# The first modulation group in two halves of the features, with two weight chunks loaded in between and the first products drawn forward

## What is computed

```
mod = silu(c) @ w_mod[i] + b_mod[i]          # six groups of 1024; c for latent tokens, c_ctx for context
h   = rmsnorm(x, g_mix_pre) * (1 + mod[1]) + mod[0]
p   = h @ w_in[i]                            # then decays, attention, Fourier mixing, convolution
```

## Time and profile before

| | |
|---|---|
| median of three runs | 1592.35 us |
| lowest, highest | 1590.29, 1592.84 us |
| the profiled execution | 1594.53 us, span 1592.7 us |
| PE busy | 1536.5 us, 96% |
| VectorE, ScalarE, POOL busy | 855.0, 571.8, 593.4 us |
| mean DMA rate | 115 GB/s |

### The profile page before, as it was taken

The page is one execution under the profiler, slowest core; times in us unless marked ns, Lnnn a source line. Parts: engine busy times, 40 slices in busy tenths (PEclk is TensorE's granted clock), DMA queues, the critical chain, the costliest instruction groups (busy, mean ns, idle before and its releaser), DMA issues.

```text
span 1592.7 us, 22922 instructions
## 1 busy us (share of the span) xinstructions
PE 1536.5 (96%) x9056; PEld 1383.9 (87%) x9056; DVE 855.0 (54%) x1309; ACT 571.8 (36%) x923; POOL 593.4 (37%) x309
## 2 busy tenths in 40 slices
PE   5999999999999999999999989999999999999997
PEld 2799999887799999999999869888898888888887
DVE  1576888637756325761366684477666332223236
ACT  4644214525544213441244255432535322222221
POOL 0532212245425525553255233332252444444441
PEclk9899999999999999999999999999999999999999
DMA  9544532255312203122121441663050333323221
GB/s 369 205 157 150 160 112 91 82 200 197 134 57 77 80 26 106 54 80 79 53 80 60 143 168 53 206 199 111 28 169 22 114 117 114 125 92 104 94 83 63
DMA packets 54062, 183.93 MB, mean 115 GB/s; under 512 B 5650, under 2 KB 10642, under 8 KB 51028
## 3 DMA queue, kind: packets, MB, share of 16 engines
q1 hardware_dynamic: 47826, 168.85, 31.5%
q10 hardware_dynamic: 6146, 13.83, 2.5%
HBM read 171.13 MB, written 11.53 MB: 115 GB/s over the span
## 4 chain that ended last, share of the span: by engine, by line
PE 90%; DVE 3%; ACT 3%; DMA 1%; POOL 1%; issue 1%; SPq 1%; ACTq 0%; DVEq 0%; POOLq 0%
PE A L1063 62%; PE A L1318 8%; PE N L1318 4%; PE G L1318 4%; PE A L1252 1%; PE A L1246 1%; PE G L1221 1%; DMA raw<-modw 1%; PE G L1373 1%; PE G L1180 1%; PE A L1214 1%; PE N L1234 1%; PE A L1260 1%; PE N L1164 1%; SPq L916 1%
## 5 line engine op out<-in xcount | busy, mean ns | idle before, releaser
L1000 POOL TENSOR_TENSOR w_lo<-raw,w_hi 128x1024 fp32r<-128x1024 f32 (+2 forms) x163 | 385.8, 2370 | 659.8 <-ACT w_hi L1400 622.0
L1063 PE MATMUL A<-h_hi,w_hi 128*128 128x512 f32 (+2 forms) x1264 | 415.1, 359 | 20.6 <-POOL h_lo L1046 11.0
L1063 PE MATMUL A<-h_hi,w_lo 128*128 128x512 f32 (+2 forms) x1264 | 404.2, 350 | 0.0
L1063 PE MATMUL A<-h_lo,w_hi 128*128 128x512 f32 (+2 forms) x1264 | 404.1, 350 | 0.0
L1400 ACT ACTIVATE w_hi<-raw 128x1024 fp32r<-128x1024 f32 (+2 forms) x163 | 167.3, 1028 | 371.4 <-PE A L1063 330.5
L1063 PEld LDWEIGHTS A<-h_hi,w_hi 128*128 128x128 f32 x1264 | 234.8, 190 | 64.4 <-POOL h_lo L1046 17.4
L1063 PEld LDWEIGHTS A<-h_hi,w_lo 128*128 128x128 f32 x1264 | 236.8, 190 | 22.0
L1063 PEld LDWEIGHTS A<-h_lo,w_hi 128*128 128x128 f32 x1264 | 236.9, 190 | 21.1 <-issue 0.5
L1063 PE MATMUL A<-g_hi,w_hi 128*128 128x384 f32 (+2 forms) x480 | 146.3, 348 | 3.8 <-DVE g_lo L1900 2.0
L1063 PE MATMUL A<-g_lo,w_hi 128*128 128x384 f32 (+2 forms) x480 | 145.2, 345 | 0.0
L1063 PE MATMUL A<-g_hi,w_lo 128*128 128x384 f32 (+2 forms) x480 | 145.1, 345 | 0.0
(11 more groups left out here) (319 smaller groups left out, 2618.6 us busy)
## 6 DMA issues: line engine op xcount, KB each, us to landing
raw<-stream SPq DMA_DIRECT2D x150, 512.0 KB, 3.7
mraw<-modv SPq DMA_DIRECT2D x54, 512.0 KB, 4.4
mraw<-modw SPq DMA_DIRECT2D x10, 1024.0 KB, 6.5
raw<-pairs SPq DMA_DIRECT2D x18, 512.0 KB, 4.7
raw<-modw SPq DMA_DIRECT2D x6, 1024.0 KB, 14.7
x<-x_keep ACTq DMA_DIRECT2D x4, 1536.0 KB, 13.6
raw<-stream SPq DMA_DIRECT2D x16, 384.0 KB, 3.1
bg<-modv SPq DMA_DIRECT2D x10, 512.0 KB, 4.0
```

The costliest lines, as they stand in the source:

```text
L1000: pool.tensor_tensor(lo, like_chunk(n, raw[:, n % RAW, 0:WIDTH[n]]), hi.bitcast(F32), ALU.subtract).then_inc(lo_done, 1)
L1063: m = pe.matmul(dst[:, at:at + t1 - t0], a, b[:, k, t0:t1], start=(first and p == 0), stop=(last and p == 2))
```

## The change

The eight 1 MB pieces of layer 0's first group become sixteen halves of 512 KB: half h holds, for one k, shift and scale of features 4h to 4h+3 (8 column tiles). Half 0 accumulates in bank G0, half 1 in N1. Each half has its own copy, two transposes and coefficients ("modh", "mturnh"). The new list takes: squares and sums of s = 0; first halves; coefficients of features 0 to 3; those features; second halves 0 to 4; products of the first projection with features 0 to 3; second halves 5 to 7; coefficients of features 4 to 7; those features; products of the second projection with features 0 to 3, of the first with 4 to 7; squares and sums of s = 1; products of the second projection with 4 to 7; features of s = 1; both projections with s = 1.

SyncE issues half 0 whole (the identity behind its second transfer), chunk 0, second halves 0 to 6, chunk 1, second half 7, the context's x. The `raw0` buffer is smaller (32 KB a partition in place of 48), the second halves go to `mraw` and to slots 2 and 3 of `w_place` and `w_sum`. ScalarE makes the high part of chunk 0 behind the first copy and that of chunk 1 behind the second; POOL makes only chunk 0's low part before feature 1, and waits for the second coefficients before chunk 1's. For features 3 and 7 VectorE writes to G0 in place of A1.

```diff
     order = [("pos", 0)]
-    order += [("sq", 0, 0, 0, k) for k in range(KT)] + [("rstd", 0, 0, 0)]
-    modk(0, 0, range(KT // 2))
-    order += [("sq", 0, 0, 1, k) for k in range(KT)] + [("rstd", 0, 0, 1)]
-    modk(0, 0, range(KT // 2, KT))
-    order += [("mturn", 0, 0)]
-    order += [("nrm", 0, 0, s, k) for s in range(2) for k in range(KT)]
-    order += [("head", -1, 1, j, s) for s in range(2) for j in range(2)]
+    sums = lambda part: [("sq", 0, 0, part, k) for k in range(KT)] + [("rstd", 0, 0, part)]
+    order += sums(0)
+    halves = lambda h, ks: [("modh", 0, h, k) for k in ks]
+    features = lambda s, ks: [("nrm", 0, 0, s, k) for k in ks]
+    order += halves(0, range(KT)) + [("mturnh", 0, 0)] + features(0, range(4))
+    order += halves(1, range(5)) + [("head", -1, 1, 0, 0, 0, 4)] + halves(1, range(5, KT)) + [("mturnh", 0, 1)]
+    order += features(0, range(4, KT)) + [("head", -1, 1, 1, 0, 0, 4), ("head", -1, 1, 0, 0, 4, KT)]
+    order += sums(1) + [("head", -1, 1, 1, 0, 4, KT)] + features(1, range(KT))
+    order += [("head", -1, 1, j, 1) for j in range(2)]
...
-            raw0 = sb("raw0", [P, KT - 2, MW], stack=first)
+            raw0 = sb("raw0", [P, KT, 1024], stack=first)
...
+        def half_at(h, k):
+
+            if h == 0:
+                return raw0[:, k, :]
+            return mraw[:, k // 2, 1024 * (k % 2):1024 * (k % 2) + 1024] if k < 4 else (w_place, w_sum)[k // 2 - 2][:, 2 + k % 2, :]
...
-            for p in range(KT):
-                if p == X_PIECES:
-                    sp.dma_start(x[:, :, SEQ:TOK], xT[:, :, SEQ:TOK]).then_inc(ctx_in, 16)
-                    sp.dma_start(ident[:, :], wide[:, 512:640]).then_inc(ident_in, 16)
-                piece(p)
+            def chunk(n):
+
+                sp.dma_start(raw[:, n % RAW, 0:WIDTH[n]], stream[n, :, 0:WIDTH[n]]).then_inc(raw_in[n % RAW], 16)
+
+            for h in range(2):
+                for k in range(KT):
+                    if (h, k) in ((1, 0), (1, KT - 1)):
+                        chunk(min(k, 1))
+                    sp.dma_start(half_at(h, k), modh[h, k]).then_inc(half_in[KT * h + k], 16)
+                    if (h, k) == (0, 1):
+                        sp.dma_start(ident[:, :], wide[:, 512:640]).then_inc(ident_in, 16)
+            sp.dma_start(x[:, :, SEQ:TOK], xT[:, :, SEQ:TOK]).then_inc(ctx_in, 16)
...
+                if e == ("nrm", 0, 0, 0, 4):
+                    pool.wait_ge(coef_step, 2)
                 if e[0] == "nrm" and e[4] not in LOW_V:
-                    asked = RAW if PLAN.n0[e] == 0 else RING if e[1] else RING - 1
+                    asked = (RAW if e[3] else 1 + e[4] // 4) if PLAN.n0[e] == 0 else RING if e[1] else RING - 1
...
+            def modulate_half(e):
+
+                _, _, h, k = e
+                unit_free(e)
+                if (h, k) == (0, 0):
+                    pe.wait_ge(csil_ready, 1)
+                pe.wait_ge(half_in[KT * h + k], 16)
+                for j in range(4):
+                    mm = pe.matmul(half_bank(h)[32 * j:32 * j + 32, :], csil[:, k, :], half_at(h, k)[:, 256 * j:256 * j + 256],
+                                   start=(k == 0), stop=(k == KT - 1))
+                mm.then_inc(half_used, 1)
...
+                elif kind == "mturnh":
+                    h = e[2]
+                    if h == 0:
+                        pe.wait_ge(ident_in, 16)
+                    pe.wait_ge(mrow_ready, MTURN[e])
+                    for b in range(2):
+                        mm = pe.transpose(half_bank(h)[:, b * P:(b + 1) * P], mrow[:, 256 * h + b * P:256 * h + (b + 1) * P],
+                                          ident[:, :])
+                    mm.then_inc(mod_turned, 1)
...
-                elif e == ("mturn", 0, 0):
-                    for j in range(RAW):
-                        high(j)
+                elif kind == "modh" and e[3] == KT - 1:
+                    h = e[2]
+                    act.wait_ge(half_used, KT * (h + 1))
+                    act.activation(mrow[:, 256 * h:256 * h + 256], half_bank(h), ACT.Copy).then_inc(mrow_ready, 1)
+                elif kind == "mturnh":
+                    high(e[2])
...
+                elif kind == "mturnh":
+                    h = e[2]
+                    unit, own = ("G0", "N1")[h], slice(4 * h, 4 * h + 4)
+                    dve.wait_ge(mod_turned, MTURN[e])
+                    src = half_bank(h).rearrange("p (m r) -> p m r", r=32)
+                    for w, v in itertools.product(range(2), range(2)):
+                        m = dve.tensor_tensor(modT[:, KT * w + 4 * h:KT * w + 4 * h + 4, v], src[:, 4 * w:4 * w + 4, v],
+                                              col(0, PB + KT * w + 4 * h, 4), ALU.add)
+                    m.then_inc(free[unit], 1)
+                    dve.wait_ge(free[unit], PLAN.before[("modh", 0, h, 0)][0][1] + 1)
+                    for v in range(2):
+                        dve.tensor_copy(coef[:, 0, 0, own, v], modT[:, own, v])
+                        m = dve.scalar_tensor_tensor(coef[:, 0, 1, own, v], modT[:, KT + 4 * h:KT + 4 * h + 4, v], 1.0,
+                                                     col(0, PG + 4 * h, 4), ALU.add, ALU.mult)
+                    m.then_inc(coef_step, 1)
+                    dve.wait_ge(coef_step, COEF[e])
...
-                    for j in ((k - 1, k) if k == KT - 1 else (k - 1,)):
+                    first = e[1:4] == (0, 0, 0)
+                    for j in ((k - 1, k) if k == KT - 1 or first and k == 3 else () if first and k == 4 else (k - 1,)):
```

More of the change, by code:

```diff
@@ L408, in __init__ @@
                 units = ["G0"]
+            elif kind == "modh" and e[3] == 0:
+                units = [("G0", "N1")[e[2]]]
             elif kind == "proj":
@@ L473 @@
 PIECE = {e: i for i, e in enumerate(PIECES)}
-MTURN = {e: i + 1 for i, e in enumerate(x for x in ORDER if x[0] == "mturn")}
-COEF = {e: i + 1 for i, e in enumerate(x for x in ORDER if x[0] in ("mturn", "mcoef"))}
+MTURN = {e: i + 1 for i, e in enumerate(x for x in ORDER if x[0] in ("mturnh", "mturn"))}
+COEF = {e: i + 1 for i, e in enumerate(x for x in ORDER if x[0] in ("mturnh", "mturn", "mcoef"))}
 TILES = [e for e in ORDER if e[0] == "dot"]
@@ L524, in piece_before @@
 def piece_before(p):
-    if PIECES[p][1:3] == (1, 0) and PIECES[p][3] < 2:
+    if p < 2:
         return PLAN.n0[("proj", 0, 19)] + RAW + RING - 1
@@ L538, in tile_before, with bass_hybrid_block @@
     return PLAN.n0[TILES[t - SLOTS]] + RAW + RING
-def bass_hybrid_block(nc: bass.Bass, stream, pairs, modw, modv, vecs, xT, pos_row, pos_col, cols, wdec, masks, mats, wide, x_keep, out):
+def bass_hybrid_block(nc: bass.Bass, stream, pairs, modh, modw, modv, vecs, xT, pos_row, pos_col, cols, wdec, masks, mats, wide, x_keep, out):
     with ExitStack() as ctx:
@@ L655, in bass_hybrid_block @@
         G = [ps("G0", 512), ps("G1", 512)]
-        first_in = [sem(f"first_in{j}") for j in range(KT - 2)]
+        half_in, half_used = [sem(f"half_in{j}") for j in range(2 * KT)], sem("half_used")
         mod_in, mod_used = [sem(f"mod_in{j}") for j in range(2)], sem("mod_used")
@@ L785, in affine_at @@
             t0, t1, _ = span(e)
+            if e[1:4] == (0, 0, 0) and e[4] in LOW_V[1::2]:
+                return G[0][:, 0:t1 - t0]
             return affine[e[4]][:, 0:t1 - t0] if ("rstd",) + e[1:4] in IN_PSUM and e[4] in LOW_V else y[:, e[4], t0:t1]
@@ L798, in piece_at, with half_bank @@
         def piece_at(p):
-            return raw0[:, p - 2, :] if 2 <= p < KT else mraw[:, p % 2, :]
+            return mraw[:, p % 2, :]
+        def half_at(h, k):
+            if h == 0:
+                return raw0[:, k, :]
+            return mraw[:, k // 2, 1024 * (k % 2):1024 * (k % 2) + 1024] if k < 4 else (w_place, w_sum)[k // 2 - 2][:, 2 + k % 2, :]
+        def half_bank(h):
+            return N[:, 512:768] if h else G[0][:, 0:256]
         def piece_in(p):
-            if 2 <= p < KT:
-                return first_in[p - 2], 16
-            return mod_in[p % 2], 16 * (1 + sum(1 for q in range(p % 2, p, 2) if not 2 <= q < KT))
+            return mod_in[p % 2], 16 * (p // 2 + 1)
         def o_at(b, h):
@@ L912, in piece @@
             def piece(p):
-                if p >= KT:
-                    sp.wait_ge(tile_used, L0_TILES)
-                    sp.wait_ge(mod_used, max(q for q in range(p) if q % 2 == p % 2 and not 2 <= q < KT) + 1)
+                sp.wait_ge(tile_used, L0_TILES)
+                if p >= 2:
+                    sp.wait_ge(mod_used, p - 1)
                 sp.dma_start(piece_at(p), modw[p]).then_inc(piece_in(p)[0], 16)
@@ L949, in tile @@
                         sp.wait_ge(chunk_used, TWICE[0, 1] + KT)
-                    sp.wait_ge(mod_used, PIECE[("modk", 1 if t else 0, 0, KT - 1)] + 1)
+                    if t:
+                        sp.wait_ge(mod_used, PIECE[("modk", 1, 0, KT - 1)] + 1)
+                    else:
+                        sp.wait_ge(half_used, 2 * KT)
                     nv = 1 if t else 2
```

(12 more changed lines are left out.)

8 lines of the change are left out of this document (2 added, 6 removed).

## The result

The changed kernel takes 1596.8 us, the median of 8 executions (1594.75 to 1598.47), against 1592.82 for the kernel before on the same chip; the ratio is 1.0025, with an interval of 1.0015 to 1.0034. It is slower, by 4.0 us (2.4 to 5.4 by the interval), where the forecast said 2.3. The forecast's time was 1594.7 us, its range 1590.8 to 1599.2. The prediction had held a difference under 3.2 us to be the likeliest outcome (0.56) and a slower kernel less likely (0.38). The profiled execution took 1596.79 us, its span is 1595.0.

What follows compares the result with a forecast made beforehand. PE bounds, 90% of the span; only its opening gaps count. Dense start -3.6, nine products done -2.0, clock -0.6, context sums +3.6, stall +3.4, z3 +1.4, rounding 0.1: +2.3 us, 1594.7 us, range 1590.8 to 1599.2.

Steps and rivals of the forecast that it cites:

- Rival (e): Loads: transfers pay by number, 2.1 us for each of eight more, last half 17 us later; 1609 us, chance 0.02.
- Rival (a): Patchy PE work from 28.5 to 33.3 us: the clock falls early; +5.5 us, 1597.8, chance 0.22.
- S: Time when the first context feature starts on VectorE, behind the context's sums and rstd; forecast 52.95 us.
- z1: Decay product whose chain waits on ScalarE for chunk 4 and whose bank z3 needs; forecast done at S+22.4.
- z3: Second decay product of the pair starting at 72.60 us in the kernel before; forecast 75.4 against 73.1.
- z3, +1.4: Term at the decay products: z3 waits for z1's bank, as chunk 4 lands late; +1.4 us.
- z0: First decay product, behind the context's last products; forecast at S+10.85 = 63.8 us, against 63.02 before.
- rival (b): Context features: the clock falls between spaced products, costing about 2.9, of which 1.4 hidden; +3.8 us, 1596.2, chance 0.12.
- the mark: Start of z3 on PE, used to measure the opening; forecast 75.4 us against 73.1 in the kernel before.
- the stall's 3.4: Term at the context features: PE waits for them, with only 12 products as cover; +3.4 us.

Runs made afterwards that it cites:

- halves_first: The changed kernel with second halves 5 to 7 and the second transposes ahead of the twelve drawn-forward products; 1596.4 us.
- fillers: The changed kernel with two useless 512-column matmuls ahead of each context feature's products, from the second on, in the first projection; 1594.89 us.
- after_wd_late: The changed kernel with decay table wd loaded as 96 rows and one, and chunk 4's high part made behind z's first exponentials; ratio 1.0024 to the kernel before.
- pool_early: The changed kernel without POOL's wait for the second coefficients, so chunk 1's low part runs beside them; 1595.48 us.
- sums_early: The changed kernel with the context's squares and sums right behind the second halves, and rstd behind the products of features 4 to 7; 1591.35 us.
- sums_wd: sums_early with the 97-row decay table wd loaded as 96 rows and one row; 1589.18 us.

## Why the prediction was right, and where it was off

**Direction** held, and most of the mechanism: the opening won about what was forecast and gave back more behind the products. The term behind them was the wrong one. The steps, in order:

- Transfers by halves cost nothing up to 33 us: 410 GB/s against 413 over the stretch of the earlier trace rows. From 33 to 35.5 the rate was 356 against 395, and the last half landed near 35.3 where I took 34.4. Why isn't known. Rival (e) is out.
- First half: eight pieces took 3.66, so 0.46 each where I took 0.435. First coefficients done at 27.8, as forecast within 0.1, which is partly luck: the halves ended 0.5 late (25.98 for 25.45), and the chain behind them took 1.8 where I took 2.25.
- Twelve products from 30.30 to 35.2 at full clock (forecast 30.1 to 34.65). Rival (a) is out for this kernel. halves_first shows that the fall was possible, with a patchier stretch; its price of 5.5 us no run shows.
- "No coefficient comes earlier for features 4 to 7 than before": second set done at 38.4 (forecast 38.1). The last half's landing sets most of it; the products' part is about 0.7 us, by the estimate at halves_first.
- The dense part from 40.91 (forecast 40.5). The clock fell at 41.2, after the gap and not in it, and was back at 44.6: 3.4 us of work at half clock, 1.7 us lost, where I took 2.3. That and the later start cancel: PE reached the context's sums at 48.10 (48.25).
- Context sums of 3.6 on PE's path: 3.62. S at 52.71 (52.95).
- Chunk 4 issued at 62.89 (S+10.2 = 62.91), z1 done at S+21.96 (S+22.4). But z3 did not wait for it: the term "z3, +1.4" of the sum measured 0.

**The step that failed** is this: PE "does the other 24 products of 256 at (62.81-57.17)/47 = 0.12 by S+10.75". That is their price at full clock. The clock fell at 58.2, behind waits of 0.76, 0.26 and 0.30 us between the features' products (a fourth, of 0.39, came in the fall), and was back at 65.0. z0 came at S+13.2, not at S+10.85, 2.4 us late, and with it z3. This is rival (b), to which I gave 0.12.

Part of these 2.4 us would have been lost to z1 in any case. fillers shows how much: with the clock kept up, the mark is won 1.4 us and z1 then binds, so 1.0 was hidden (rival (b) had 1.4). after_wd_late shows the other side: with z1 out of the way and the clock still falling, nothing is won.

Whether the fall could have been forecast stays open. The earlier trace rows had a stretch with waits of the same kind behind which the clock was lost (951.1), and it was lost here in the changed kernel, in pool_early and in after_wd_late alike. But halves_first has almost the same waits at the same features and kept full clock; it differs in what PE did before, working from 37.2 on where the changed kernel idles until 40.91. So the waits alone do not decide it, and no run here shows what does. The Trainium skill, "TensorE: Matmul & The Clock Gate", section "HAM oscillation — how this bites in real kernels", tells of waits between bursts behind each of which the clock is lost again. The runs agree with it in the changed kernel, where it was lost twice in 25 us, and not in halves_first.

In numbers, the mark moved by 76.08 - 73.13 = 2.95 (2.3 forecast). That the two are this near is luck in part: the 1.4 for z3 was not there, and the 2.4 of the half clock, which the sum had at nothing, stood in its place. Rival (b) had 3.8: it took 2.9 for the half clock, which measured 2.4, and S came 0.24 early. The profiled executions are 2.3 us apart, the medians 4.0, because the profiled one of before was 1.7 above its median (2.2 above the median of the three runs known then), while the changed kernel's is at its median. The forecast took the same 2.2 off for the changed kernel, which is why its time of 1594.7 came out 2.1 too low although its 1596.8 for the profiled execution was met. Executions of the kernel before do differ: of the 27 beside the last three kernels, nine took 1589.8 to 1590.8 and eighteen 1592.3 to 1593.7. The stretches at half clock near 877, 955 and 1548 us come and go from profile to profile, at 1.5 to 3.4 us lost in each. That they make these two groups is likely by their size, but isn't shown, since there is one profile of that kernel.

**What made it a loss** is one part of the change, the context's sums behind the products. They used to fill a wait; moved, they cost 3.6 us of PE, leave a gap behind which the clock falls, and leave the chain of the context's features, 7.5 us, with 12 products over it. sums_early shows it: with the eight sums in the gap the mark is 5.4 us earlier and the loss of 4.0 us is gone. How the 5.4 divides among the sums, the clock and the cover no run separates, except for the second fall's 1.4 (fillers). I had listed their 3.6 and the stall's 3.4 separately, and never asked what the rest of the change would be worth without them.

## What to carry to other kernels

When work is drawn forward, look at what it leaves for the next chain of small dependent steps: here the products that were done early were the cover of the context's features. Put work that depends on nothing into the gaps ahead of the dense part, where in sums_early it also kept the clock up, and price every stretch in which PE waits between short bursts at half clock as well as at full. An edit can be worth nothing until another has moved the bound: the late chunk and the split table won nothing in the kernel before or in the changed one, and 4.2 us once PE came early. And follow the clock past the stretch that was changed: in sums_early and halves_first it fell right behind the mark.

## What was not expected of the hardware

VectorE's copy of 4 columns, 0.17 us by itself, took 2.29, 2.31 and 2.31 us beside a running POOL tensor_tensor of 2.35, and ended as it ended. The Trainium skill has it ("SBUF — State Buffer", section "Who interferes with whom"): a copy may use the port pair that VectorE shares with GpSimd, and whoever starts second waits for the whole instruction of the other. The traces agree: POOL's instruction kept its usual 2.3 to 2.4 and only the copy, which started second each time, was longer. The changed kernel escapes it by POOL's wait for the second coefficients.

A load of 97 rows at 25 GB/s also went with a longer transfer behind it: chunk 4 took from its issue at 56.59 until ScalarE had it at 62.17 with wd in flight (sums_early), and from 56.03 to 59.19 with wd split (sums_wd).
